# A diffusion-layer kernel: channel sums of a LayerNorm moved to GpSimd, and another order of VectorE's steps in the ConvFFN pairs

## The reference

```python
u = depthwise_conv(u_a * sigmoid(u_b), cdw_w, cdw_b)          # width 31
u = silu(layer_norm(u, cln_w, cln_b))                         # mean and variance over 1024 channels
conv_out = u @ conv_w_out
mixed = sigmoid(gate_ret) * ret_out + sigmoid(gate_conv) * conv_out
x = x + g1 * rms_norm(mixed @ w_mix_out, n1_post)
h2 = rms_norm(x, n2_pre) * (1 + sc2) + sh2
up = depthwise_conv(h2 @ ffn_w_up, fdw_w, fdw_b)              # width 3, 2 x 2816 channels
a, gl = split(up, 2)
x = x + g2 * rms_norm((silu(a) * gl) @ ffn_w_down, n2_post)
```

## Time and profile before

| | |
|---|---|
| median of 3 runs | 2301.18 us (2299.71 to 2301.8) |
| profiled execution, its time | 2302.16 us |
| its span | 2300.1 us |
| TensorE matmul busy | 2203.3 us, 96% |
| VectorE busy | 1533.7 us, 67% |
| GpSimd busy | 928.4 us, 40% |
| ScalarE busy | 773.7 us, 34% |

### The profile page before, as it was taken

One profiled execution on the slowest core, in us unless ns is written; L12 is line 12 of the kernel. 1 busy time (PEld: TensorE's weight loads), 2 busy tenths in 40 slices (PEclk: granted clock), 3 DMA queues, 4 the chain that ended last, 5 costly groups with the idle time before them and its releaser, 6 DMA issues.

```text
span 2300.1 us, 31642 instructions
## 1 busy us (share of the span) xinstructions
PE 2203.3 (96%) x12566; PEld 2011.6 (87%) x12566; DVE 1533.7 (67%) x1757; ACT 773.7 (34%) x1303; POOL 928.4 (40%) x602
## 2 busy tenths in 40 slices
PE   5899999999999899999999999989999999999998
PEld 2789989988988899999889998889999999978887
DVE  2479388388389467676435445587778777766776
ACT  2311101201201256665537233343333333344342
POOL 0314314314313266665211121055555555565654
PEclk9899999999999999999999999999999999999999
DMA  8333333333332445545544444312222121275653
GB/s 274 110 115 116 93 119 116 109 108 111 95 104 93 144 144 169 161 149 151 186 134 129 130 149 161 110 29 86 59 65 79 58 86 58 70 289 204 204 181 125
DMA packets 246545, 291.77 MB, mean 127 GB/s; under 512 B 12193, under 2 KB 198913, under 8 KB 246401
## 3 DMA queue, kind: packets, MB, share of 16 engines
q1 hardware_dynamic: 175553, 219.23, 29.7%
q10 hardware_dynamic: 69440, 65.82, 8.8%
q0 software_dynamic: 1408, 4.72, 0.5%
HBM read 222.71 MB, written 67.01 MB: 126 GB/s over the span
## 4 chain that ended last, share of the span: by engine, by line
PE 71%; DVE 12%; ACT 5%; issue 5%; POOL 4%; DMA 2%; SPq 0%; ACTq 0%; DVEq 0%; POOLq 0%
PE ps L906 70%; DVE f_cv L2390 6%; POOL f_cv L1959 3%; ACT f_cv L1721 2%; DVE f_in L2423 2%; DVE E L2399 1%; POOL O_lo L1954 1%; ACT f_cv L1727 1%; DMA ada_p<-in_ada_w 1%; PE ps L1062 1%; DVE T_raw L2351 1%; DVE E L2402 1%; ACT f_in L1324 0%; DVE A_lo L2054 0%; DVE A_hi L2053 0%
## 5 line engine op out<-in xcount | busy, mean ns | idle before, releaser
L2071 DVE SCALAR_TENSOR_TENSOR conv_y<-u_in,VC,conv_y 128x1167 f32<-128x1167 f32 x240 | 406.6, 1694 | 7.4
L1834 POOL TENSOR_TENSOR Wa_lo<-W_raw,Wa_hi 128x1024 fp32r<-128x1024 f32 x58 | 146.5, 2531 | 496.2 <-ACT Wa_hi L1324 495.9
L906 PE MATMUL ps<-A_hi,Wa_hi 128*128 128x384 f32 x768 | 265.5, 346 | 4.9 <-ACT hf L1365 4.1
L906 PE MATMUL ps<-A_lo,Wa_hi 128*128 128x384 f32 x768 | 263.5, 343 | 0.0
L906 PE MATMUL ps<-A_hi,Wa_lo 128*128 128x384 f32 x768 | 263.2, 343 | 0.0
L2390 DVE SCALAR_TENSOR_TENSOR f_cv<-f_in,VF,f_cv 128x1023 f32<-128x1023 f32 (+1 forms) x176 | 220.7, 1314 | 50.8 <-ACT f_cv L1721 50.6
L1834 POOL TENSOR_TENSOR D_lo<-F_raw,D_hi 128x1024 fp32r<-128x1024 f32 x66 | 162.4, 2464 | 97.9 <-ACT D_hi L1324 97.9
L2427 DVE TENSOR_TENSOR g_lo<-g_raw,g_hi 128x384 fp32r<-128x384 f32 x66 | 138.5, 2108 | 82.0 <-ACT g_hi L1324 82.0
L1954 POOL TENSOR_TENSOR O_lo<-E,O_hi 128x512 fp32r<-128x512 f32 x80 | 129.0, 1613 | 153.8 <-ACT O_hi L1324 153.8
L906 PE MATMUL ps<-Wb_hi,A_hi 128*128 128x512 f32 x432 | 171.7, 398 | 0.0
L906 PE MATMUL ps<-Wb_lo,A_hi 128*128 128x512 f32 x432 | 171.1, 396 | 0.0
(11 more groups left out here) (286 smaller groups left out, 5521.6 us busy)
## 6 DMA issues: line engine op xcount, KB each, us to landing
F_raw<-in_ffn_w_down SPq DMA_DIRECT2D x66, 512.0 KB, 3.7
F_raw<-in_ffn_w_up SPq DMA_DIRECT2D x44, 512.0 KB, 5.5
qt<-qkvg_d SPq DMA_DIRECT2D x36, 512.0 KB, 3.8
W_raw<-in_w_in SPq DMA_DIRECT2D x32, 512.0 KB, 4.5
W_raw<-in_w_in SPq DMA_DIRECT2D x64, 256.0 KB, 3.2
ada_w<-in_ada_w ACTq DMA_DIRECT2D x32, 512.0 KB, 5.0
g_d<-f_cv SPq DMA_DIRECT2D x22, 576.0 KB, 3.0
g_raw<-g_d SPq DMA_DIRECT2D x66, 192.0 KB, 3.7
```

The costliest lines, as they stand in the source:

```text
L906: return pe.matmul(out, l, r, start=start, stop=stop)
L1834: return pool.tensor_tensor(dst, x, Fv(hi), ALU.subtract)
L2071: dve.scalar_tensor_tensor(out=y, in0=x, scalar=tap, in1=y, op0=ALU.mult, op1=ALU.add).then_inc(q.conv_step, 1)
```

## The change

Three edits. In the merge the 8 channel tiles are first added by GpSimd (4 + 4, 2 + 2, 1 + 1, into c_sq), and TensorE does one product for each mean and each variance. The tables give every step of the LayerNorm another tile, and ScalarE does its square and root steps ahead of the chunk's high part and gate, the silu behind them. In the pairs VectorE's steps stand in another order, the side taps in halves, and GpSimd makes S4's low part ahead of `product(j-1)`. The loads of x2 use the semaphores of xt instead of two of their own.

```diff
-        LN_MEAN, LN_VAR = {2: 0, 5: 1, 8: 2}, {6: 0, 9: 1, 13: 2}
-        LN_DVE = {3: [("centre", 0)], 6: [("centre", 1), ("eps", 0)], 8: [("scale", 0)], 9: [("centre", 2), ("eps", 1)],
-                  11: [("scale", 1)], 13: [("split", 0), ("eps", 2)], 15: [("scale", 2)], 17: [("split", 1)], 20: [("split", 2)]}
-        LN_ACT = {4: [("square", 0)], 6: [("square", 1), ("root", 0)], 8: [("silu", 0)], 9: [("square", 2), ("root", 1)],
-                  11: [("silu", 1)], 13: [("root", 2)], 15: [("silu", 2)]}
+        LN_MEAN, LN_VAR = {5: 0, 6: 1, 8: 2}, {11: 0, 13: 1, 15: 2}
+        LN_DVE = {6: [("centre", 0)], 7: [("centre", 1)], 9: [("centre", 2)], 12: [("eps", 0)], 13: [("scale", 0)], 14: [("eps", 1)],
+                  16: [("eps", 2), ("scale", 1)], 18: [("scale", 2)], 19: [("split", 0)], 21: [("split", 1)], 23: [("split", 2)]}
+        LN_ACT = {6: [("square", 0)], 7: [("square", 1)], 9: [("square", 2)], 12: [("root", 0)], 13: [("root", 1)],
+                  14: [("silu", 0)], 16: [("root", 2)], 17: [("silu", 1)], 20: [("silu", 2)]}
+        LN_POOL = {0: [("mean", 2)], 1: [("square", 0), ("square", 1)], 2: [("square", 2)]}
...
             def ln_mean(g):
-                pe.wait_ge(cr_in[g], 32)
+                pe.wait_ge(q.ln_sum, 3 * LN_SUM_MEAN[g])
                 if g:
                     pe.wait_ge(q.ln_dve, ln_done["centre", g - 1])
                 tok = slice(g * TG, (g + 1) * TG)
-                for k in range(KT):
-                    last = mm(ps[:, 6, 0:TG], mean_w[:, :], c_raw[:, k, tok], k == 0, k == KT - 1)
-                last.then_inc(q.ln_pe, 1)
+                mm(ps[:, 6, 0:TG], mean_w[:, :], c_sq[:, 0, tok], True, True).then_inc(q.ln_pe, 1)
...
@@ scalar @@
+            for n in range(8):
+                steps_ = [x for e in range(NTG * n, NTG * n + NTG) for x in LN_ACT.get(e, ())]
+                for what, g in steps_:
+                    if what != "silu":
+                        ln_step[what](g)
+                split_m(n + 3)
+                gate_sig(n + 2)
+                for what, g in steps_:
+                    if what == "silu":
+                        ln_step[what](g)
...
@@ gpsimd @@
+            def ln_tree(what, g):
+                tok = slice(g * TG, (g + 1) * TG)
+                if what == "mean":
+                    pool.wait_ge(cr_in[g], 32)
+                else:
+                    pool.wait_ge(q.ln_act, ln_done["square", g])
+                src = c_raw if what == "mean" else c_sq
+                for n_ in (4, 2, 1):
+                    if n_ < 4:
+                        pool.wait_ge(q.ln_sum, sums[0])
+                        src = c_sq
+                    pool.tensor_tensor(c_sq[:, 0:n_, tok], src[:, 0:n_, tok], src[:, n_:2 * n_, tok], ALU.add).then_inc(q.ln_sum, 1)
+                    sums[0] += 1
+            ln_tree("mean", 0)
+            ln_tree("mean", 1)
             for n in range(16):
                 if n + 3 < 16:
                     lo_m(n + 3)
-                elif n == 14:
+                for what, g in LN_POOL.get(n, ()):
+                    ln_tree(what, g)
+                if n == 14:
                     lo_m(16)
...
                 op_lo(op_no(j, U_A12))
+                op_lo(op_no(j, U_S4))
                 product(j - 1)
-                op_lo(op_no(j, U_S4))
...
@@ vector @@
+            s_last(PLAIN)
             for j in range(PLAIN, FKT):
-                if j > PLAIN:
-                    ev(j - 1, EV_C12)
-                    side_taps(j - 1, 0)
-                s_last(j)
                 ev(j, EV_U2)
                 ev(j, EV_U3)
                 ev(j, EV_C21)
                 if j + 1 < FKT:
                     s_first(j + 1)
                 ev(j, EV_C22)
                 ev(j, EV_A2)
+                ev(j, EV_C11)
                 if j + 1 < FKT:
-                    side_taps(j, 1)
-                ev(j, EV_C11)
+                    side_taps(j, 1, (0,))
+                    ev(j, EV_C12)
+                    side_taps(j, 1, (1,))
+                    side_taps(j, 0, (0,))
+                    s_last(j + 1)
+                    side_taps(j, 0, (1,))
```

More of the change, by code:

```diff
@@ L392, in build @@
         q.ln_pe = sem("ln_pe")
+        q.ln_sum = sem("ln_sum")
         q.cr_hi_ok = sem("cr_hi_ok")
@@ L437, in build @@
         rT_s = [q.rT_s0, q.rT_s1]
-        x2_in = [sem("x2_in0"), sem("x2_in1")]
         cr_in = [sem(f"cr_in{g}") for g in range(NTG)]
@@ L586, in build @@
         VAR_1, MO, X2, VAR_2, XN2 = 1, 2, 3, 4, 5
-        LN_MEAN, LN_VAR = {2: 0, 5: 1, 8: 2}, {6: 0, 9: 1, 13: 2}
-        LN_PE_MEAN, LN_PE_VAR = (1, 2, 4), (3, 5, 6)
-        LN_DVE = {3: [("centre", 0)], 6: [("centre", 1), ("eps", 0)], 8: [("scale", 0)], 9: [("centre", 2), ("eps", 1)],
-                  11: [("scale", 1)], 13: [("split", 0), ("eps", 2)], 15: [("scale", 2)], 17: [("split", 1)], 20: [("split", 2)]}
-        LN_ACT = {4: [("square", 0)], 6: [("square", 1), ("root", 0)], 8: [("silu", 0)], 9: [("square", 2), ("root", 1)],
-                  11: [("silu", 1)], 13: [("root", 2)], 15: [("silu", 2)]}
+        LN_MEAN, LN_VAR = {5: 0, 6: 1, 8: 2}, {11: 0, 13: 1, 15: 2}
+        LN_PE_MEAN, LN_PE_VAR = (1, 2, 3), (4, 5, 6)
+        LN_DVE = {6: [("centre", 0)], 7: [("centre", 1)], 9: [("centre", 2)], 12: [("eps", 0)], 13: [("scale", 0)], 14: [("eps", 1)],
[3 more added lines that the diff above has]
+        LN_POOL = {0: [("mean", 2)], 1: [("square", 0), ("square", 1)], 2: [("square", 2)]}
+        LN_SUM_MEAN, LN_SUM_SQ = (1, 2, 3), (4, 5, 6)
         ln_done = {}
@@ L597, in build @@
             ln_done.update({x: n + 1 for n, x in enumerate(made)})
+        XT_LAST = (16 * 5, 16 * 4)
         MIX_ORDER = [(0, 0), (1, 0), (0, 1), (1, 1)] + [(t, half) for t in range(2, NT) for half in range(2)]
@@ L891, in _ @@
                     if t >= 2:
-                        sp.wait_ge(x2_in[t % 2], 16 * (t // 2))
-                    sp.dma_start(x2t[:, t, :], x2_d[t]).then_inc(x2_in[t % 2], 16)
+                        sp.wait_ge(xt_in[t % 2], XT_LAST[t % 2] + 16 * (t // 2))
+                    sp.dma_start(x2t[:, t, :], x2_d[t]).then_inc(xt_in[t % 2], 16)
                 if p and k in (14, 16, 18):
@@ L1179, in ln_mean @@
                 tok = slice(g * TG, (g + 1) * TG)
-                for k in range(KT):
-                    last = mm(ps[:, 6, 0:TG], mean_w[:, :], c_raw[:, k, tok], k == 0, k == KT - 1)
-                last.then_inc(q.ln_pe, 1)
+                mm(ps[:, 6, 0:TG], mean_w[:, :], c_sq[:, 0, tok], True, True).then_inc(q.ln_pe, 1)
             def ln_var(g):
-                pe.wait_ge(q.ln_act, ln_done["square", g])
+                pe.wait_ge(q.ln_sum, 3 * LN_SUM_SQ[g])
                 if g:
@@ L1188, in ln_var @@
                 tok = slice(g * TG, (g + 1) * TG)
-                for k in range(KT):
-                    last = mm(ps[:, 7, 0:TG], mean_w[:, :], c_sq[:, k, tok], k == 0, k == KT - 1)
-                last.then_inc(q.ln_pe, 1)
+                mm(ps[:, 7, 0:TG], mean_w[:, :], c_sq[:, 0, tok], True, True).then_inc(q.ln_pe, 1)
             for n in range(16):
@@ L1639, in _ @@
             gate_sig(1)
-            for n in range(16):
+            for n in range(8):
[8 more added lines that the diff above has]
+                        ln_step[what](g)
+            for n in range(8, 16):
                 if n + 3 < 16:
@@ L1647, in _ @@
                 for e in range(NTG * n, NTG * n + NTG):
[L1648 to L1651, removed]
+                    m_part(e)
                 if n + 2 < 16:
@@ L1936, in _ @@
                 gate_w(x)
+            sums = [0]
+            def ln_tree(what, g):
[13 more added lines that the diff above has]
+            ln_tree("mean", 1)
             for n in range(16):
@@ L2377, in _, with side_taps @@
             B_lo_part(NT - 1)
-            def side_taps(j, kind):
+            def side_taps(j, kind, which=(0, 1)):
                 n0 = tap_no(j, kind) - 4
                 dve.wait_ge(q.fc0, c0_no(j, kind))
-                for n, w in enumerate((0, 2)):
+                for n in which:
+                    w = 2 * n
                     for piece_, (lo, hi) in enumerate(((0, LAT), (LAT, T))):
@@ L2492, in e_apply @@
                                               op0=ALU.mult, op1=ALU.mult))
-                dve.wait_ge(x2_in[n % 2], 16 * (n // 2 + 1))
+                dve.wait_ge(xt_in[n % 2], XT_LAST[n % 2] + 16 * (n // 2 + 1))
                 dve.tensor_tensor(x2t[:, n, :], x2t[:, n, :], y_t[n % 4][:, :], ALU.add).then_inc(q.e_o, 1)
```

## The result

The changed kernel takes 2251.49 us (median of 4 runs, 2251.09 to 2251.79) against 2301.49 us (4 runs, 2299.71 to 2302.99): a ratio of 0.978, 95% interval 0.9768 to 0.9791. The prediction was 2252.5. Its profiled execution took 2251.79 us.

The account below looks back on a forecast made before the run. TensorE bounds the merge; in the pairs a loop of the other engines stalls it 1.48 us a pair. Merge 21.5 plus pairs 27.2 plus end 0 gives 48.7 us off 2302.16, less 0.98: 2252.5 us, range 2246 to 2268.

Parts of the forecast that it names:

- End: Start of the down projection: later first loads of g cost 0, with 1.5 us to either side.
- Rival A: The forecast: TensorE bounds merge and pairs, one stall at mean 1; 2252.5 us, chance 0.50.
- stall: Merge: TensorE waits 4.2 us at the mean of group 1 until VectorE has evicted group 6 and centred group 0.
- clock: Merge: after the wait at mean 1 TensorE runs at the 1.2 GHz level for a while, costing 1.5 us.
- The trees' cover: Merge: GpSimd's additions for each mean or variance finish in time, with 6 us of cover or more for each.
- the floor: Pairs: TensorE's 168 products take 22.4 us a pair, which sets the pace once the other engines' loop is shorter.
- step (1): Pairs: S4's low part ahead of product(j-1) on GpSimd changes the loop by -0.6 us, or +0.6 at the bad end.
- steps (2) and (3): Pairs, VectorE's order: moving C11 and C12 takes 0.7 and 1.4 us off the loop; s_last entering it adds 0.65.
- Rival B: Pairs: the shared port keeps the loop above TensorE, period 22.7 to 23.2 us; 2258 to 2267 us, chance 0.26.
- rival D: Pairs gain nothing: product(j-1) ahead of s_first costs as much as the order saves; 2279.7 us, chance 0.07.
- Rival E: Pairs: VectorE locks GpSimd out, S3's low part comes late and the kernel gets slower; 2325 us, chance 0.04.
- Rival C: Merge: the wait at mean 1 does not arise or takes no clock; 2247 to 2251 us, chance 0.10.

Follow-up runs that it names:

- merge_only: The merge's edits alone, with the pairs' lines of the kernel before: 2280.63 us, 0.9905 of the kernel before.
- pairs_only: The pairs' edits alone, put into the kernel before, merge as before: 2272.80 us, 0.9869 of the kernel before.
- mean_early: The changed kernel with the mean of group 0 asked for one tile earlier and its centring after tile 5: 2246.44 us, 0.9757 of the kernel before.
- eight_products: The changed kernel with TensorE's eight products for each mean and variance again, no sums on GpSimd: 2280.40 us, 0.9905 of the kernel before.
- pool_old: The changed kernel with GpSimd's product(j-1) back ahead of S4's low part, VectorE's new order kept: 2251.18 us, 0.9776 of the kernel before.
- dve_old: The changed kernel with VectorE's whole old order in the pairs, GpSimd's new order kept: 2288.71 us, 0.9938 of the kernel before.

## Why the prediction was right

**The sum.** 48.7 us were forecast for the span, 50.2 came. By stage: merge 21.5 forecast, 21.1 in the trace and 21.9 by merge_only. Pairs 27.2 forecast, 30.8 in the trace with 2.3 of them at the start of the down projection, so 28.5, and 30.1 by pairs_only. End 0 forecast, 2.3 - 1.65 = 0.7 in the trace. Rival A, the forecast, was what happened, with two errors in the pairs' loop that cancelled.

**Merge.** Right in each term: six sums 27.2 forecast, 26.9 by mean_early's chain; stall 4.2, measured 4.10, at 1167.4 with the releaser named; clock 1.5, measured 1.6; together 5.7, 5.8 by mean_early. A tree 6.4, measured 6.5. The first tile of the convolution branch came 21.2 us earlier (1247.16 against 1268.31), 21 forecast. The trees' cover held, which eight_products confirms from the other side.

**Pairs, the floor.** Right: 22.40 us a pair, no wait in the pairs after the 0.69 us at S1 of pair 3, so it costs nothing that VectorE falls in step with TensorE. (That it does so at C11's product was argued; no run separates it.) Of the pairs' 1.3 us above the forecast 0.8 came ahead of the steady pairs: from the ConvFFN's restart to S1 of pair 3 it is 80.46 us before (1576.23 - 1495.77) and 79.07 after (1553.78 - 1474.71), 1.4 us where the sum had 0.6.

**Pairs, step (1), wrong.** I had GpSimd's edit end s_first at 8.1 instead of 8.7 us after p1_copy, -0.6, and named 9.3 as the bad end. It ends at 9.1, against 8.8 in the trace before (1607.49 + 0.68), and the loop is 0.3 us longer, in both rows of the table. The sentence that failed is "So E1 waits for the product, ends at 6.9, and s_first at 8.1". E1 does wait, to 1658.34 - 1651.57 = 6.8; but A11's low part then takes the next turn, between E1 and E3. I had the mechanism and nearly the number, and chose the wrong end: GpSimd had an instruction queued, and here it took its turn.

**Pairs, steps (2) and (3), too small.** -1.5 forecast (-0.7 - 1.4 + 0.65), -2.2 measured. In today's trace a half of the side taps takes 2.54 us with GpSimd's instructions in between, and I kept that for all four. After the change they take 2.58, 4.40 for two, and 1.53, which is 8.5 us instead of 10.1. Only s_last, 1.78 instead of 0.68, pays some back. That makes 0.5 of the 0.7. The two errors, +0.9 and -0.7, nearly cancelled: 21.8 forecast, 21.93 measured. That the loop came out right was luck, and the kernel's time would not have shown the difference: any loop under 22.4 gives TensorE's pace.

**Gain for the floor.** Since both loops with VectorE's new order are under 22.4, GpSimd's edit changes no time here (pool_old). Without the other edit it costs 8 us (dve_old), 5 of them in the loop. Rival B, the port holding the loop above TensorE, failed by a margin of 0.5 us a pair (21.93 against 22.40); rival D's mechanism is real (GpSimd's edit does cost), but at 0.3 us a pair it is far below the 2.2 that VectorE's order gives. Rival E did not occur: no wait for O_lo in the steady pairs. Rival C was excluded by the stall. The 30.1 us of pairs_only are above the 28.5 + 0.7 of the change's trace because it kept what it gained at g_lo: 1.9 us less waiting there, and no slow clock behind D_lo (241.27 us for the last 1062 products against 242.81).

**The end.** I took 0 for the first loads of g. TensorE's wait shrank by 2.3 us; I had said that p1_copy might be ahead of TensorE by then, which fits, but no run tests it. Of the 2.3, 1.65 came back behind the wait for D_lo, as slow clock, which I had not looked at. That 0 was nearly right is luck as well: mean_early, with the same wait of 2.44 us, kept its clock.

## What to carry to other kernels

When two engines hold each other up instruction by instruction, count what is queued behind the instruction that runs. Moving one step ahead of another on GpSimd can delay VectorE although the wanted step comes earlier. To see a loop that the bound engine hides, take work away from that engine: the loop's own period then stands in the trace, and here edits of 0.3 us showed in it that the kernel's time could not show. When a table says after which tile an engine does what, check each pair of tables for a step placed exactly where the other engine is about to wait for it; here one place in a table cost 5.8 us. When a wait grows, look at the time from the restart before it to the restart behind it: here that time had not changed, and the loss stood behind the wait, in the clock.

## What the runs showed of the hardware

VectorE and GpSimd held each other up, and in the pairs they alternated: in dve_old the product of 2.67 us, E1, A11's low part, E3, in that order, each VectorE instruction ending 0.55 us after GpSimd's. The Trainium skill, "SBUF — State Buffer", section "SBUF: two separate sides", states that of a VectorE instruction with two SBUF inputs and a GpSimd instruction the one that starts first has the shared ports for its whole length, and the other is blocked. The trace agrees (E1 3.04 us, 0.70 alone). Who comes next when both have work queued is what these runs add, and it is not always the other engine. Before the change GpSimd's product of 11.60 us began at 1520.29, while VectorE went from instruction to instruction until 1529.43:

```profile
1526.87 2.56 DVE L2351 TENSOR_TENSOR T_raw<-T_raw,B_lo 128x2304 f32<-128x2304 f32 x1
```

The product ended 2.46 us after that, and elsewhere it takes 2.7: there GpSimd got no turn. What decides between the two is open.

TensorE's granted clock was at its 1.2 GHz level after the wait of 4.10 us at 1171.52 (0.50), after the one of 3.98 us before the change, and after the one of 2.44 us at 1987.05 (0.51). Each cost 1.6 to 1.7 us more than the wait itself. After a wait of the same 2.44 us at the same place in mean_early it stayed at 1.00, so the length of the wait alone did not decide it.
